# A hybrid decoder layer on one core: each block's rows spread over the partitions, x for the tail loaded and scaled ahead of the last expert results, the norms' affine part in two passes

## The reference, cut to what matters

```python
x = layer_norm(DN_ALPHA * x + mix, ln1_g, ln1_b)                 # LN1
ffn = hier_moe(x, ...)       # top-1 of 4 groups, top-2 of its 8 experts, SwiGLU experts:
                             # (silu(xb @ w_gate[e]) * (xb @ w_up[e])) @ w_down[e], times gates, summed over the 2
x = layer_norm(DN_ALPHA * x + ffn, ln2_g, ln2_b)                 # LN2
ple = sigmoid(x @ w_ple_gate) * (p @ w_ple_proj)
x = x + rms_norm(ple, ple_norm_g)

def layer_norm(x, g, b):
    xc = x - mean(x); var = mean(xc * xc)
    return xc * rsqrt(var + LN_EPS) * g + b
```

## Time and profile before

| | us |
|---|---|
| median of 3 runs | 1042.96 |
| profiled execution, its own time | 1042.33 |
| its span, first to last instruction | 1040.6 |
| TensorE busy | 937.9 (90%) |
| VectorE busy | 422.9 (41%) |
| ScalarE busy | 244.1 (23%) |
| GpSimd busy | 94.4 (9%) |

### The profile page before, as it was taken

The page is one execution under the profiler, slowest core; times in us unless marked ns, Lnnn a source line. Parts: engine busy times, 40 slices in busy tenths (PEclk is TensorE's granted clock), DMA queues, the critical chain, the costliest instruction groups (busy, mean ns, idle before and its releaser), DMA issues.

```text
span 1040.6 us, 13802 instructions
## 1 busy us (share of the span) xinstructions
PE 937.9 (90%) x5204; PEld 562.2 (54%) x5204; DVE 422.9 (41%) x934; ACT 244.1 (23%) x515; POOL 94.4 (9%) x143
## 2 busy tenths in 40 slices
PE   7999988999989989999899998889999987950996
PEld 6777766777767755665588444443333332320442
DVE  0211387565543247668512344452111111113773
ACT  0122121032224015766600000211111110101344
POOL 0111211211112000000000000011111111110000
PEclk9999998999999999999999999889999998995899
DMA  9766885996967500101125942329999999977001
GB/s 377 283 232 244 308 298 200 319 349 236 361 224 249 225 26 19 44 20 38 66 102 222 423 205 106 137 72 409 425 419 427 422 423 426 408 307 251 1 21 61
DMA packets 61221, 244.08 MB, mean 235 GB/s; under 512 B 10738, under 2 KB 11507, under 8 KB 51683
## 3 DMA queue, kind: packets, MB, share of 16 engines
q1 hardware_dynamic: 42818, 189.04, 46.6%
q0 software_dynamic: 13152, 35.28, 9.4%
q10 hardware_dynamic: 5184, 18.88, 4.8%
HBM read 239.69 MB, written 14.87 MB: 245 GB/s over the span
## 4 chain that ended last, share of the span: by engine, by line
PE 72%; DMA 14%; DVE 8%; ACT 3%; issue 2%; SPq 1%; ACTq 0%; DVEq 0%; POOLq 0%
PE ps L768 17%; DMA arena<-in_wexp 10%; PE ps L1180 8%; PE ps L1068 5%; PE ps L1111 5%; PE ps L1265 3%; PE ps L1200 3%; PE ps L856 3%; PE ps L761 3%; PE ps L827 3%; PE ps L937 2%; DMA arena<-in_state 2%; DVE arena L1747 2%; PE ps L961 2%; PE ps L1130 1%
## 5 line engine op out<-in xcount | busy, mean ns | idle before, releaser
L768 PE MATMUL ps<-arena 128*128 128x260 f32 x960 | 223.7, 389 | 6.1 <-DMA arena<-in_w 6.1
L768 PEld LDWEIGHTS ps<-arena 128*128 128x128 f32 x960 | 181.4, 193 | 40.7 <-issue 8.5
L1180 PE MATMUL ps<-arena 128*64 128x512 f32 x576 | 129.4, 602 | 16.0 <-DMA arena<-in_wexp 14.5
L1180 PEld LDWEIGHTS ps<-arena 128*64 128x64 f32 x576 | 42.7, 139 | 90.3 <-issue 88.4
L1599 DVE SCALAR_TENSOR_TENSOR arena<-arena,vec 128x512 f32<-128x512 f32 x120 | 81.9, 745 | 0.0
L2169 POOL DMA_DIRECT2D arena<-in_kv x96 | 51.7, 539 | 285.9 <-issue 279.8
L1200 PE MATMUL ps<-arena 128*64 128x512 f32 x288 | 65.8, 598 | 3.8 <-DMA arena<-in_wexp 3.0
L2053 DVE TENSOR_TENSOR arena<-ps,arena 128x256 f32<-128x256 f32 x18 | 7.6, 425 | 140.2 <-ACT arena L1464 140.2
L1068 PE MATMUL ps<-arena 128*128 128x260 f32 x256 | 56.3, 383 | 0.7 <-issue 0.7
L1111 PE MATMUL ps<-arena 128*128 128x512 f32 x128 | 56.1, 595 | 0.0
L1068 PEld LDWEIGHTS ps<-arena 128*128 128x128 f32 x256 | 48.7, 191 | 8.2 <-issue 1.0
(11 more groups left out here) (307 smaller groups left out, 1138.1 us busy)
## 6 DMA issues: line engine op xcount, KB each, us to landing
arena<-in_wexp SPq DMA_DIRECT2D x32, 2048.0 KB, 23.6
arena<-in_kv SPq DMA_DIRECT2D x160, 272.0 KB, 8.8
arena<-in_wexp SPq DMA_DIRECT2D x32, 1024.0 KB, 25.8
arena<-in_kv POOLq DMA_DIRECT2D x96, 272.0 KB, 7.0
arena<-in_w ACTq DMA_DIRECT2D x36, 512.0 KB, 7.0
arena<-in_wo SPq DMA_DIRECT2D x8, 512.0 KB, 3.8
arena<-in_w_out SPq DMA_DIRECT2D x4, 1024.0 KB
arena<-in_w_plg SPq DMA_DIRECT2D x1, 4096.0 KB, 15.0
```

The lines of the kernel that those rows point to most:

```text
L768: y = mm(ps[:, b + h, 0:TH], w[:, k], xT[:, k, h * TH:(h + 1) * TH], start=(k == 0), stop=(k == KD - 1))
L1180: y = mm(ps[64 * x:64 * x + 64, 2, :], xgT[:, k, 64 * x:64 * x + 64], wx[slot][:, x, k * 512:(k + 1) * 512], start=(k == 0), stop=(k == KD ...
```

## The change

- The rank of a pair no longer is its place in the block: the constant `CROW`, in place of `CEID`, gives rank r the place 8 * (r % 8) + (r // 8 + r % 8) % 8. Ranks 0 to 7 stand on places 0, 9, 18, 27, 36, 45, 54 and 63, ranks 8 to 15 on 1, 10, 19, 28, 37, 46, 55 and 56.
- `fx` moves from slot W0 to W2, `yl` from W2 to W0. So `fx` is loaded once the pair in W2 has been used, one pass before the end, with a semaphore of its own. ScalarE scales it by alpha (`scaled`) in place of `first_choice`, and VectorE adds both results times their gates to it. The loops for further blocks use slot 0 alone.
- `norm` subtracts the mean and multiplies by the gain in one pass, ahead of the wait for the root, and multiplies by rstd and adds the bias in a second one.
- ScalarE takes a root of a constant, whose result is not used, at the start of the tail and before the last tile's second sum of squares.

```diff
--- before.py
+++ after.py
@@ -113,9 +113,9 @@
 N_INI = 7
 N_NRM = 4 + 5 + 3
 CONV_STEPS = KC * CW
-LN_STEPS, FD = 10, 8
+LN_STEPS, FD = 10, 7
 R_EXP, R_EXP2, R_RANK, R_IDX, R_IDS, R_STEPS = 12, 17, 21, 46, 50, 61
-HF_STEPS = 9
+HF_STEPS = 8
 SCALE = float((NOPE + ROPE) ** -0.5)
 ALPHA = float(2.0 ** 0.25)
 LN_EPS, RMS_EPS = 1e-5, 1e-6
@@ -135,7 +135,8 @@
 CSV = CSEL + P
 CSUM = CSV + 2 * P
 CRQ = CSUM + 16
-NCON = CRQ + 1
+CROW = CRQ + 1
+NCON = CROW + CAP
 
 VQG, VKG, VBD, VLG, VLB, VDW = 0, 3, 5, 9, 13, 17
 NVEC = VDW + KC * CW
@@ -210,16 +211,16 @@
 
 A_PLG = A_W1
 A_ROWS = A_W1 + 8192
-A_FX = A_W0
+A_FX = A_W2
 A_FBT = A_FX + TILES * D
 A_SG = A_FBT + 2 * D
-A_OUT = A_SG + 2 * D
-A_SQF = A_OUT + 2 * D
-assert A_SQF + D <= A_W0 + 2 * EW
-A_YL = A_W2
-A_NP = A_YL + 2 * TILES * D
+A_SQF = A_SG + 2 * D
+A_NP = A_SQF + D
 A_PZ = A_NP + D
 assert A_PZ + D <= A_W2 + 2 * EW
+A_YL = A_W0
+A_OUT = A_YL + 2 * TILES * D
+assert A_OUT + 2 * D <= A_W0 + 2 * EW
 ARENA = max(A_END1, A_W0 + 2 * EW)
 
 
@@ -486,6 +487,7 @@
         s_ovd = sem("s_ovd")
         s_yl = [sem(f"s_yl{t}") for t in range(TILES)]
         s_g0 = sem("s_g0")
+        s_fxl = sem("s_fxl")
         s_hf = sem("s_hf")
         s_hr = sem("s_hr")
         s_ht = sem("s_ht")
@@ -528,7 +530,7 @@
             return p % 3, p // 3 + 1
 
 
-        OV_SLOT, OV_LOADS = (2, 0), (5, 6)
+        OV_SLOT, OV_LOADS = 0, sum(k % 3 == 0 for k in range(EPAIRS))
 
         def narrow(bank, rows32, w):
 
@@ -687,16 +689,20 @@
             sp.wait_ge(m.y, LAST_USE[EPAIRS - 3] + 1)
             sp.dma_start(plg[:], a["w_plg"]).then_inc(s_plg, 16)
             sp.dma_start(ln2r[:], a["lnrows"][:, 2:4]).then_inc(s_plg, 16)
+            sp.wait_ge(m.y, LAST_USE[EPAIRS - 2] + 1)
+            for u, t in enumerate(ORDER):
+                sp.wait_ge(s_x1[u], 16)
+                sp.dma_start(fx[0:ROWS[t], t], x1d[t * P:t * P + ROWS[t]]).then_inc(s_fxl, 16)
             sp.wait_ge(s_r, R_STEPS)
             blocks = sp.value_load(ovi[0:1, 16:17], min_val=0, max_val=OVB)
 
             def weights(p, s, i):
-                sp.wait_ge(m.y, p - 1)
+                sp.wait_ge(m.y, p)
                 sp.sem_inc(s_own, 1)
                 for x in range(2):
                     e = sp.value_load(ovi[0:1, bass.ds(2 * (p - NPASS) + x, 1)], min_val=0, max_val=NEXP - 1)
                     for down in range(2):
-                        expert_weights(OV_SLOT[s], x, e, down)
+                        expert_weights(OV_SLOT, x, e, down)
 
             overflow(sp, blocks, weights)
             sp.wait_ge(s_ovd, 1)
@@ -706,7 +712,6 @@
                 n = ROWS[t]
                 for k in range(2):
                     sp.dma_start(yl[0:n, t, k], ybd[k * T + t * P:k * T + t * P + n]).then_inc(s_yl[u], 16)
-                sp.dma_start(fx[0:n, t], x1d[t * P:t * P + n]).then_inc(s_yl[u], 16)
             for u, t in enumerate(ORDER2):
                 sp.wait_ge(s_fy, u + 1)
                 sp.dma_start(o["y"][t * P:t * P + ROWS[t]], yo[0:ROWS[t], u % 2]).then_inc(s_yo[u % 2], 16)
@@ -1221,11 +1226,11 @@
             blocks = pe.value_load(ovi[0:1, 16:17], min_val=0, max_val=OVB)
 
             def extra(p, s, i):
-                loaded = 32 * (i + OV_LOADS[s] + 1)
+                loaded = 32 * (2 * i + s + OV_LOADS + 1)
                 rows_in(p, s, 16 * (i + NPASS // 2 + 1))
-                gate_up(p, OV_SLOT[s], loaded)
+                gate_up(p, OV_SLOT, loaded)
                 turn_h(p)
-                down(p, OV_SLOT[s], loaded)
+                down(p, OV_SLOT, loaded)
 
             overflow(pe, blocks, extra)
             pe.wait_ge(s_ovd, 1)
@@ -1487,11 +1492,10 @@
 
             overflow(act, blocks, extra)
 
-            def first_choice(u):
+            def scaled(u):
                 t = ORDER2[u]
                 n = ROWS[t]
-                act.wait_ge(s_yl[u], 48)
-                av(yl[0:n, t, 0], yl[0:n, t, 0], ACT.Copy, scale=gates[0:n, 0, t:t + 1]).then_inc(s_g0, 1)
+                av(fx[0:n, t], fx[0:n, t], ACT.Copy, scale=ALPHA).then_inc(s_g0, 1)
 
             def root(u):
                 n = ROWS[ORDER2[u]]
@@ -1520,16 +1524,15 @@
                 act.wait_ge(s_hs, 2 * u + 1)
                 av(rms[0:n, 1:2], rms[0:n, 0:1], ACT.Sqrt, bias=eps[0:n, 0:1], scale=1.0 / D).then_inc(s_hs, 1)
 
-            act.wait_ge(s_ovd, 1)
-            for u in range(3):
-                first_choice(u)
+            av(rms[:, 5:6], eps[:, 0:1], ACT.Sqrt)
+            act.wait_ge(s_fxl, 16 * TILES)
+            for u in range(TILES):
+                scaled(u)
             root(0)
             turned(0)
             root(1)
             turned(1)
             root(2)
-            first_choice(3)
-            first_choice(4)
             sigmoid(0)
             turned(2)
             squares(0)
@@ -1547,6 +1550,8 @@
             for h in range(2):
                 act.wait_ge(s_h, TILES + h)
                 av(sg[:, 0, 512 * h:512 * (h + 1)], ps[:, h, :], ACT.Sigmoid).then_inc(s_hg, 1)
+                if h == 1:
+                    av(rms[:, 5:6], eps[:, 0:1], ACT.Sqrt)
                 act.wait_ge(s_pm, TILES + h)
                 av(sqf[:, 512 * h:512 * (h + 1)], sg[:, 0, 512 * h:512 * (h + 1)], ACT.Square,
                    accum_out=rms[:, 3 + h:4 + h]).then_inc(s_hs, 1)
@@ -1866,14 +1871,14 @@
                     v.bn_stats(bst[0:n, hh], x[:, hh * 512:(hh + 1) * 512]).then_inc(stats_sem, 1)
                 dve.wait_ge(stats_sem, base + 2)
                 v.bn_aggr(mv[0:n], bst[0:n].rearrange("p h s -> p (h s)")).then_inc(stats_sem, 1)
+                dve.wait_ge(stats_sem, base + 3)
+                v.scalar_tensor_tensor(out=x, in0=x, scalar=mv[0:n, 0:1], in1=g[0:n], op0=ALU.subtract,
+                                       op1=ALU.mult).then_inc(stats_sem, 1)
                 dve.wait_ge(root_sem, root_n)
                 v.reciprocal(rstd[0:n, 1:2], rstd[0:n, 0:1]).then_inc(stats_sem, 1)
-                dve.wait_ge(stats_sem, base + 4)
-                v.tensor_scalar(x, x, mv[0:n, 0:1], rstd[0:n, 1:2], ALU.subtract, ALU.mult).then_inc(stats_sem, 1)
                 dve.wait_ge(stats_sem, base + 5)
-                v.tensor_tensor(x, x, g[0:n], ALU.mult).then_inc(stats_sem, 1)
-                dve.wait_ge(stats_sem, base + 6)
-                v.tensor_tensor(x, x, b[0:n], ALU.add).then_inc(stats_sem, 1)
+                v.scalar_tensor_tensor(out=x, in0=x, scalar=rstd[0:n, 1:2], in1=b[0:n], op0=ALU.mult,
+                                       op1=ALU.add).then_inc(stats_sem, 1)
 
             def logits(u):
                 t = ORDER[u]
@@ -2002,7 +2007,7 @@
             v.tensor_copy(slotb, slotx[:, 1])
             step(v.tensor_copy(slotr, slotx[:, 0]))
             dve.wait_ge(s_f, TILES)
-            io = con[:, CEID:CEID + CAP].unsqueeze(1).to_broadcast([P, 2 * TILES, CAP])
+            io = con[:, CROW:CROW + CAP].unsqueeze(1).to_broadcast([P, 2 * TILES, CAP])
             v.tensor_tensor(inrow.rearrange("p k t r -> p (k t) r"), io,
                             slotr.rearrange("p k t -> p (k t)").unsqueeze(2).to_broadcast([P, 2 * TILES, CAP]),
                             ALU.is_equal).then_inc(s_rt2, 1)
@@ -2085,15 +2090,13 @@
                 t, b = ORDER2[u], HF_STEPS * u
                 n = ROWS[t]
                 x = fx[0:n, t]
-                dve.wait_ge(s_yl[u], 48)
+                dve.wait_ge(s_yl[u], 32)
                 dve.wait_ge(s_g0, u + 1)
                 y = yl[0:n, t]
-                v.scalar_tensor_tensor(out=y[:, 0], in0=y[:, 1], scalar=gates[0:n, 1, t:t + 1], in1=y[:, 0],
-                                       op0=ALU.mult, op1=ALU.add).then_inc(s_hf, 1)
-                dve.wait_ge(s_hf, b + 1)
-                v.scalar_tensor_tensor(out=x, in0=x, scalar=ALPHA, in1=y[:, 0], op0=ALU.mult,
-                                       op1=ALU.add).then_inc(s_hf, 1)
-                dve.wait_ge(s_hf, b + 2)
+                for k in range(2):
+                    v.scalar_tensor_tensor(out=x, in0=y[:, k], scalar=gates[0:n, k, t:t + 1], in1=x,
+                                           op0=ALU.mult, op1=ALU.add).then_inc(s_hf, 1)
+                    dve.wait_ge(s_hf, b + k + 1)
                 norm(n, x, s_hf, b + 2, s_hr, u + 1, ln2r[:, 0], ln2r[:, 1])
 
             def gated(u):
@@ -2258,6 +2261,9 @@
     for t in range(TILES):
         con[:, CTOK + t] = t * P + q - FREE
         con[:, CTOK + TILES + t] = T + t * P + q - FREE
+
+    r = np.arange(CAP)
+    con[:, CROW + 8 * (r % 8) + (r // 8 + r % 8) % 8] = r
     con[:, CVAL] = (TILES - 1) * P + q < T
     con[:, CBLK:CBLK + 16] = NEXP + TWICE - 1 + np.arange(16)
     for j in range(4):
```

## The result

| | us |
|---|---|
| median after, 4 runs | 1029.82 (1027.15 to 1030.77) |
| median before, 4 runs beside them | 1042.19 (1040.09 to 1043.85) |
| ratio after / before | 0.9881, 95% interval 0.986 to 0.9902 |
| profiled execution, its own time; span | 1027.15; 1025.4 |
| the same kernel again beside the last three variants, 6 runs | 1030.21 (1026.94 to 1032.01), ratio 0.9884 [0.9864, 0.9904] |

A forecast was written before the change was run, and what follows sets the result against it. The prediction took the expert stage to be bound by the weights' transfer. VectorE's earlier start 8.8, tile 0's norms 3.8, the gap 1.15 and the end 0.2 sum to 13.95 us: from 1042.33 to 1028.4, 1029 as median, range 1023 to 1036.

The forecast's parts named there:

- TensorE's start of the last gate/up: End of the expert stage: 6 us less transfer lag brings the last gate/up weights from 914.95 to 909.
- LN1: Last tile's first norm, ahead of the logits: two passes instead of three save 1.1 us on the path.
- The size of the lag: Last engine's finish behind the average one at the expert stage's end: falls from 9.6 to 3.7 us, bounds 0 and 9.6.
- The step that failed: Last scatter, issued at 925.9, lands in 4 to 5 us instead of 8.23, so y's loads issue at about 930.5.
- Part 3: Loads of x ahead of y: first tile ready at 942.9 instead of 949.29; a y issue at 935.5 is still covered.
- VectorE's start: Start of tile 0 in the tail: 8.8 us earlier than 950.58, including 1.1 us from the last tile's first norm.
- Tile 0's norms: First tile of the tail on VectorE: 6.9 us instead of 10.7, saving 3.8, with 3.0 us of reciprocal wait gone.
- The gap at tile 2: TensorE's 1.77 us wait for tile 2's norm in the tail: 1.15 us of it goes.
- The end: Last tile's norm: table load moved ahead of the last sum of squares leaves some 0.2 us, bounds -0.3 and 1.3.
- The lag stays: Rival: spreading rows leaves the engines' 9.6 us lag at the expert stage's end; 1035 us as median, chance 0.20.
- The slower rival: Spreading deals rows worse to the transfer engines; before's time reached at a 17.6 us lag, 1050 at 25; chance 0.05.
- Its signs: Expected in the changed profile: five timing marks; a lag above 8 us or x below 300 GB/s holding y would refute.

The follow-up runs named there:

- a1: The kernel before with only the places of the ranks (`CROW`) changed; 1035.81 us, ratio 0.9955 to before.
- a4: The changed kernel with the ranks back in their old places; 1035.74 us, ratio 0.9951 to before.
- b1: The changed kernel with ranks 0 to 7 piled on places 0 to 3 and 32 to 35, later ranks on the next; 1043.61 us, ratio 1.003.
- a2: The kernel before with only the new two-pass `norm`; 1038.11 us, ratio 0.9967 to before.
- c3: The changed kernel with six unused constant matmuls before the tail's first turn and three ahead of each of two late gate/up passes; 1027.59 us, ratio 0.9853.
- c4: The changed kernel with the 8-row loads of tile 4 put later in SyncE's order; 1029.98 us, ratio 0.9878 to before.
- b2: The changed kernel with the five loads of x behind the wait for the last scatters instead of ahead; 1034.24 us, ratio 0.9932 to before.
- b3: The changed kernel with eleven unused constant matmuls on TensorE ahead of the tail's first turn; 1032.21 us, ratio 0.991 to before.
- c1: The changed kernel as it stands, run again beside three variants; 1030.21 us, ratio 0.9884 to before.
- c2: The changed kernel with six unused constant matmuls on TensorE ahead of the tail's first turn; 1027.91 us, ratio 0.9858 to before.
- a3: The kernel before with only the new slots, early loads of x, its scaling on ScalarE and early tables; 1038.00 us, ratio 0.9971.

## Why the prediction was right, and where it was not

- **TensorE's start of the last gate/up.** 909 less 1.1 from LN1, so 907.9; it was 907.36. Counted from the first gate/up it moved by 5.3 us where 6 less lag had been counted. The mechanism, rows dealt unevenly to the engines, is shown by a1, a4 and b1.
- **The size of the lag.** 3.7 forecast; by idle shares 5.5 in a1 and 3.5 after, and no run tells how much of a1's 5.5 is the late issue of its last scatter. Judged by the landing, 245.7 to 240.2, it fell by 5.5 where 5.9 had been forecast. By the fixed owners of the Trainium skill, page "DMA: Bandwidth & Descriptors", section "The descriptor swizzle", the forecast gave lags of 12.8 and 4.5 us; at its own 0.155 us a move, 105 and 79 rows against a mean of 65 make 12.4 and 4.3. An estimate of 4.3 fits what is left as well as the 3.7 does, but a fall of 8.1 us is further from the 5.5.
- **The step that failed: "Landing took 8.23 us with the lag; 4 to 5 without, so SyncE can issue the loads of y at about 930.5".** It took 7.48, and SyncE issued at 934.6. No kernel had less than 6.24. The term counted from the scatter's issue, but the moment is set by the fuller half's backlog: counted from the first gate/up, a2 issues its scatter 1.5 us later than the kernel before (935.82 - 696.83 = 239.0 against 931.84 - 694.36 = 237.5), and it lands at 245.5 against 245.7. (The issue is not without effect once x stands in front: c3 issues 2.5 us sooner than after and lands 1.4 sooner.) Had the term been made of its own two numbers, the average engine at 930.4 - 1.1 and a lag of 3.7, it would have said 933.0. It cost nothing that can be seen, as Part 3 had said of a late issue, because queued work bridges it: x was forecast to be through at 935.6 on the average engine and had landed on the last one at 937.4, 2.8 us behind the issue.
- **VectorE's start.** 941.8 forecast, 940.80 measured; the first gate/up alone was 1.2 us earlier than forecast. Between the marks it is 7.5 us against the 8.8 - 1.1 = 7.7 of the sum; since a2, with nothing changed in this stage, stands at 254.5 where before stands at 256.2, the 7.5 is known to about 1.7 us. The covers held: the five scalings ended 1.5 us behind VectorE's start and 2.7 us ahead of the root. The 1 us for the 8-row loads was 0.4 (c4).
- **LN1.** VectorE from the sum to the logits' copies, after: 643.53 to 649.02, 5.5 us; before 643.47 to 650.14, 6.7. The 1.1 is there. The rest of the 2.3 us at the first gate/up moves from execution to execution.
- **Tile 0's norms.** 6.9 forecast, 6.8 measured; a2 alone has 7.2 with 0.39 at the reciprocal, so of the 3.8 us, 3.5 are the passes' own order and the root's cover, where a2's expectation had given them 2.0. The early table load and the early scaling, to which the forecast gave the 3.0 us of waiting, are worth only the 0.4 that is left once the norm is changed.
- **The gap at tile 2.** 1.77 became 0.66, 1.15 had been forecast to go. TensorE, after:

```profile
981.23 1.09 PE L1245 MATMUL ps<-con,arena 128*128 128x128 f32 x8 [0.66 <-DVE arena L1880]
```

- **The end.** From the last sigmoid to the last pass 3.5 us (1017.57 to 1021.04) instead of 3.9: 0.4 against 0.2 forecast.
- **What I had not counted.** The clock in the last gate/up (2.8 us longer, hidden behind the transfers) and at the tail's start. There the clock was 0.50 before as well, so no term changed, but 2.3 us more were to be had.
- **The rivals.** "The lag stays" was 1035; a4 is that case and measured 1035.74. The slower rival came true as a mechanism in b1: at a lag of more than 17.6 us before's time was to be reached, and b1's scatter landed 13.3 us later than after's; with 3.5 to 5.5 us left there, that is a lag of 17 to 19 us, an estimate.
- **Its signs.** Of what was to show it, the last gate/up near 908, VectorE's start near 942, the tile in 7 us without a wait and the gap below 0.8 came. The fall of the share within about 4 us did not (0.70 and 0.55 from 928 to 936), nor the landing in under 5.5 us (7.48). And the last part of x came at 248 and 210 GB/s, with y behind it: by its words that was to make the forecast wrong, if it held y. The start still came where it was forecast, since a low mean rate while some engines are through and others are not is the lag itself, and the lag is in the sum.

The profiled execution after was the fastest of its four, so the 15.2 us between the two profiles are more than the 12.4 of the ratio; the forecast of 13.95 lies between.

## What to carry to other kernels

When a stage is bound by transfers, look at the mean DMA share just behind its last bytes: if it falls in steps over 10 us or more while one more transfer is still awaited, the engines were not dealt equal shares, and which partitions hold the live rows of a half-filled indirect transfer is then a lever that costs no instruction. Cost a landing by the moment at which the fullest engine is through, rather than by a length from its issue. And before a slow clock is mended, ask whether the engine is on the path: of two slow stretches only the one behind which nothing but TensorE stood paid.

## What the runs showed of the hardware

- Which engine carries a row of an indirect gather or scatter depends on its partition. Three orders of the same rows, in kernels otherwise alike, put the last landing at 242.5 (after), 247.0 (a4) and 255.8 us (b1).
- Behind waits of 3.1 to 3.4 us for weights the last gate/up's 32 matmuls took 8.78 to 9.90 us in nine executions (after, a1, a2, a4, b2, b3, c1, c2, c4) and 7.09 in two, both with a wait of 3.40 (before, and a3), where the granted clock stayed at 1.00. In the four of 9.81 to 9.90 (after, b3, c2, c4) it had fallen to 0.50 during the wait; in the five of 8.78 and 8.79 it fell within the first 0.8 us of the pass. The Trainium skill, page "TensorE: Matmul & The Clock Gate", section "HAM oscillation — how this bites in real kernels", describes such falls between groups of matmuls; these runs agree, and show that waits of nearly one length can have either outcome.
- A scatter issued behind 5.2 us of loads from another queue was only 0.8 to 2.4 us late (1.1 with the same issue, c1 and b2) and landed ahead of them (934.54 and 937.4 after).
